# A decoder layer's last stage: late rows' gathers issued behind the second bulk tile, meta rows left out of the bulk, sample rows normed in sixteen pieces

## The reference

```
x = x + mixer(rmsnorm(x))                 # RWKV-7 branch, retention branch, w_out
x = x + hier_moe(rmsnorm(x))              # top-1 of 4 groups, then top-2 of its 4 experts
y = x * rsqrt(mean(x*x, -1) + 1e-6) * final_norm_g
return y[16:528], y[528:536], states      # the meta rows' y is dropped
```

## Time and profile before

| | us |
|---|---|
| median of 3 runs | 918.35 (917.46 to 920.85) |
| the profiled execution | 917.91 |
| its span, first to last instruction | 916.2 |
| last scatter-add to x issued | 876.40 |
| gathers of late rows issued | 884.13, 885.50, 886.83 |
| first sum of late rows starts (DVE) | 897.64 |
| PE's last matmul ends | 903.18 |
| last sum of late rows ends | 905.58 |
| last scatter to y issued | 911.23 |

### The profile page before, as it was taken

One profiled execution on the slowest core, in us unless ns is written; L12 is line 12 of the kernel. 1 busy time (PEld: TensorE's weight loads), 2 busy tenths in 40 slices (PEclk: granted clock), 3 DMA queues, 4 the chain that ended last, 5 costly groups with the idle time before them and its releaser, 6 DMA issues. The chain is left out here.

```text
span 916.2 us, 20394 instructions
## 1 busy us (share of the span) xinstructions
PE 854.0 (93%) x8958; PEld 599.6 (65%) x8958; DVE 376.7 (41%) x735; ACT 206.9 (23%) x427; POOL 37.6 (4%) x34
## 2 busy tenths in 40 slices
PE   8999999999999999999989989999999819999993
PEld 6877777788867766777767767766788613333330
DVE  6343334428955655444533324325511162111126
ACT  2101112033133232032123133212003230111125
POOL 0000000000000000000000000000000010222223
PEclk9999999999999999999999999999999958999998
DMA  9211111311311111110011201008272089999965
GB/s 355 107 46 46 47 46 47 150 48 70 112 47 49 55 36 38 36 37 29 26 35 49 94 26 47 28 2 299 86 298 92 0 283 415 396 395 393 391 221 208
DMA packets 27015, 118.75 MB, mean 130 GB/s; under 512 B 5344, under 2 KB 7648, under 8 KB 22064
## 3 DMA queue, kind: packets, MB, share of 16 engines
q1 hardware_dynamic: 22608, 106.51, 30.5%
q0 software_dynamic: 4320, 10.95, 4.1%
HBM read 104.17 MB, written 18.05 MB: 133 GB/s over the span
## 5 line engine op out<-in xcount | busy, mean ns | idle before, releaser
L884 PE MATMUL psum<-arena 128*128 128x268 f32 x1600 | 397.9, 397 | 2.7 <-ACT arena L1262 2.5
L884 PEld LDWEIGHTS psum<-arena 128*128 128x128 f32 x1600 | 295.4, 190 | 74.3 <-issue 7.9
L1453 DVE TENSOR_TENSOR arena<-psum,arena 128x256 f32<-128x256 f32 (+7 forms) x230 | 99.3, 437 | 280.5 <-PE psum L1201 57.8
L1262 ACT ACTIVATE arena<-psum 128x268 f32<-128x268 f32 (+9 forms) x181 | 72.7, 411 | 452.7 <-PE psum L884 280.3
L1453 DVE TENSOR_TENSOR arena<-arena 128x268 f32<-128x268 f32 (+10 forms) x203 | 102.0, 502 | 54.8 <-ACT arena L1262 43.4
L1201 PE MATMUL psum<-arena 128*128 128x268 f32 x384 | 90.3, 390 | 0.9 <-DVE arena L1453 0.9
L1998 PE MATMUL psum<-arena 128*32 128x512 f32 (+1 forms) x640 | 87.9, 613 | 2.9 <-DVE arena L2151 2.9
L1201 PEld LDWEIGHTS psum<-arena 128*128 128x128 f32 x384 | 71.3, 189 | 16.3 <-DVE arena L1453 1.7
L2151 DVE TENSOR_TENSOR arena<-psum,arena 128x256 f32<-128x256 f32 (+1 forms) x36 | 24.1, 691 | 109.6 <-ACT arena L2065 101.6
L1998 PEld LDWEIGHTS psum<-arena 128*32 128x32 f32 (+1 forms) x640 | 25.6, 118 | 61.7 <-issue 60.1
L1912 POOL DMA_INDIRECT arena<-u_rows,ids x12 | 12.4, 1036 | 809.7 <-DVE ids L2187 747.0
(11 more groups left out here) (190 smaller groups left out, 687.9 us busy)
## 6 DMA issues: line engine op xcount, KB each, us to landing
arena<-in_w_gu SPq DMA_DIRECT2D x16, 2048.0 KB, 20.7
arena<-in_w_in SPq DMA_DIRECT2D x46, 512.0 KB, 3.5
arena<-in_w_dn SPq DMA_DIRECT2D x16, 1024.0 KB, 18.7
arena<-in_w_out SPq DMA_DIRECT2D x2, 2048.0 KB, 11.9
arena<-in_x SPq DMA_DIRECT2D x8, 268.0 KB, 4.3
arena<-in_x SPq DMA_DIRECT2D x1, 2144.0 KB, 15.1
arena<-in_rets SPq DMA_DIRECT2D x1, 2048.0 KB, 15.9
out_rets<-arena SPq DMA_DIRECT2D x1, 2048.0 KB, 6.5
```

Source lines behind the costliest of these rows:

```text
L884: last = mm(ps, wt[:, i % NW, k, :], rhs[:, k, cols(hf)], start=(k == 0), stop=(k == nk - 1))
L1262: run(nc.scalar.activation(out, in_, fn, **kw), s)
L1453: run(v.tensor_tensor(out, a, b, op), s)
```

## The change

- Before the late gathers, POOL waits for the load of bulk tile 1.
- The bulk is rows 16 to 527 in four full tiles; tile 4 is now the 8 sample rows, each cut into 16 pieces of 64, so 128 partitions x 64. Its sum of squares is made per piece by ACT and added over the 16 pieces by one small matmul on PE with a block matrix `blk` (ones where two partitions belong to one row), into a column of bank 5, from which ACT takes the root. `blk` is made by DVE in `rt_in`; the matching pieces of final_norm_g come by one more load.
- The orders of squares (0, 1, 4, 2, 3, 5, 6, 7), of roots and norms (0, 1, 2, 3, 4, 5, 6, 7) and of the steps among them change, as below. The semaphore between the tiny table activations goes, and one of these (Sqrt, the third).
- POOL scatters tile 5 to y before `back(2)`.

```diff
@@ mixer: SP, ACT and DVE
+            sp.dma_start(g_smp, I["gfrow"][0:NB].rearrange("b (q c) -> (b q) c", q=16)).then_inc(d_ld, 16)
-                    act.wait_ge(d_ld, 48)
+                    act.wait_ge(d_ld, 64)
-                    dve.wait_ge(d_ld, 48)
+                    dve.wait_ge(d_ld, 64)
                     tt(quad, ident[:, 0:20], ident[:, 32:52], ALU.add)
+                    run(v.tensor_reduce(cnt, ident.rearrange("p (a b) -> p a b", a=NB), AX.X, ALU.add))
+                    run(v.tensor_copy(blk.rearrange("p (a b) -> p a b", a=NB), bc(cnt, P // NB)))
+                    run(v.memset(cnt, 0.0))
@@ final norm
+        SQUARED = [0, 1, 4, 2, 3, TT, TT + 1, TT + 2]
+        NORMED = [0, 1, 2, 3, 4, TT, TT + 1, TT + 2]
+        def bulk(t):
+            return xf[:, t, :] if t < TT - 1 else xf[:, t, 0:D // 16]
+        def bulk_rows(rows, t):
+            if t < TT - 1:
+                return rows[META + t * P:META + (t + 1) * P, :]
+            return rows[TP:T, :].rearrange("b (q c) -> (b q) c", q=16)
@@ SP
-                        n = rows_of(t)
-                        sp.dma_start(xf[0:n, t, :], x2_dram[t * P:t * P + n, :]).then_inc(z_x[t], 16)
+                        sp.dma_start(bulk(t), bulk_rows(x2_dram, t)).then_inc(z_x[t], 16)
@@ POOL
+                    then(z_x[1], 16, 16)
                     for j in range(LATE):
                         e = FIRST_LATE + j
                         pool.indirect_dma_start(late[:, j, :], None, x2_dram,
-                    for j in range(LATE):
+                    for j in range(LATE - 1):
                         back(j)
                     then(z_out[0], 48, 48)
                     then(z_out[1], 32, 32)
                     for j in range(LATE):
-                        then(z_y, TT + LATE, TT + j + 1)
+                        if j == 1:
+                            back(LATE - 1)
+                        then(z_y, TT + LATE, NORMED.index(TT + j) + 1)
@@ PE
                     hidden_in(NPASS - 1)
+                    at_least(pe, z_ss, TT + LATE, SQUARED.index(TT - 1) + 1)
+                    mm(bank(5)[:, 6 * NPASS:6 * NPASS + 1], blk, fs[:, TT - 1:TT], start=True, stop=True).then_inc(z_smp, 1)
                     down(NPASS - 2)
@@ ACT
-                    table(ACT.Sqrt)
+                    a(dummy, eps2[:, :], ACT.Sqrt)
                     for t in range(2):
                         square(t)
                         root(t)
-                    table(ACT.Sigmoid)
+                    a(lnx_eps, eps2[:, :], ACT.Sigmoid)
                     gate(NPASS - 1)
                     hidden_out(NPASS - 2)
-                    table(ACT.Sqrt)
+                    square(4)
                     square(2)
+                    hidden_out(NPASS - 1)
                     root(2)
-                    hidden_out(NPASS - 1)
-                    for t in range(3, TT + 2):
+                    square(3)
+                    root(3)
+                    root(4)
+                    for t in range(TT, TT + LATE - 1):
                         square(t)
                         root(t)
@@ DVE
                     summed(0)
                     normed(2)
                     normed(3)
+                    normed(4)
+                    normed(TT)
                     summed(1)
-                    normed(4)
+                    normed(TT + 1)
                     for q in range(2):
...
-                    for t in range(TT, TT + LATE):
-                        normed(t)
+                    normed(TT + LATE - 1)
```

More of the change, by code:

```diff
@@ L654, in hybrid_step @@
         assert top[0] <= base
+        blk = at(P)
+        g_smp = at(D // 16)
+        assert top[0] <= base
         top[0] = ug0
@@ L669, in hybrid_step @@
         u2b = at(2 * D, 2, D)
-        assert top[0] <= base, top[0] - base
+        assert top[0] <= ug0 + 4 * D
         oneb = E(nc.sbuf_tensor("oneb", [P, P], BF16))
@@ L1823, in hybrid_step @@
         z_x = [sem(f"z_x{t}") for t in range(TT)]
-        z_sq = sem("z_sq")
+        z_smp = sem("z_smp")
         z_ss = sem("z_ss")
@@ L1885, in _ @@
                     for t in range(TT):
-                        n = rows_of(t)
-                        sp.dma_start(xf[0:n, t, :], x2_dram[t * P:t * P + n, :]).then_inc(z_x[t], 16)
+                        sp.dma_start(bulk(t), bulk_rows(x2_dram, t)).then_inc(z_x[t], 16)
                     for t in range(TT):
-                        at_least(sp, z_y, TT + LATE, t + 1)
+                        at_least(sp, z_y, TT + LATE, NORMED.index(t) + 1)
                         sp.nop(nofuse=True)
-                        n = rows_of(t)
-                        sp.dma_start(O["y"][t * P:t * P + n, :], xf[0:n, t, :]).then_inc(z_out[t % 2], 16)
+                        sp.dma_start(bulk_rows(O["y"], t), bulk(t)).then_inc(z_out[t % 2], 16)
                     for j in range(LATE):
@@ L2080, in rows_out @@
                         a(yo[:, e % 2, :], psum[:, o:o + 1024], ACT.Copy, scale=w_s[:, e:e + 1]).then_inc(q_yo, 1)
-                    squares = [0]
+                    squares = []
                     def square(t):
-                        x = xf[0:rows_of(t), t, :] if t < TT else late[:, t - TT, :]
-                        n = x.shape[0]
+                        x = bulk(t) if t < TT else late[:, t - TT, :]
                         if t < TT:
@@ L2090, in square @@
                             at_least(act, z_add[t - TT], 1, 1)
[L2091 to L2096, removed]
-                    def root(t):
[L2099 to L2102, removed]
+                        if squares:
+                            at_least(act, z_ss, TT + LATE, len(squares))
+                        a(junk[:, 0:x.shape[1]], x, ACT.Square, scale=D ** -0.5, accum_out=fs[:, t:t + 1]).then_inc(z_ss, 1)
+                        squares.append(t)
+                        assert squares == SQUARED[:len(squares)]
+                    roots = []
+                    def root(t):
+                        roots.append(t)
+                        assert roots == NORMED[:len(roots)]
+                        if t == TT - 1:
+                            at_least(act, z_smp, 1, 1)
+                        else:
+                            at_least(act, z_ss, TT + LATE, SQUARED.index(t) + 1)
+                        a(rs[:, t:t + 1], bank(5)[:, 6 * NPASS:6 * NPASS + 1] if t == TT - 1 else fs[:, t:t + 1], ACT.Sqrt,
+                          bias=eps2[:, :]).then_inc(z_rt, 1)
                     for i in range(NPASS - 2):
@@ L2134, in _ @@
                     at_least(act, z_half, 1, 1)
-                    at_least(act, z_ss, TT + LATE, squares[0])
+                    at_least(act, z_ss, TT + LATE, len(squares))
                     a(junk[:, 0:512], x[:, 0:512], ACT.Square, scale=D ** -0.5,
@@ L2217, in hidden @@
                         tt(hh, b[:, FF:2 * FF], hh, ALU.mult, q_h)
-                    norms = [0]
+                    norms = []
                     def normed(t):
-                        norms[0] += 1
-                        x = xf[0:rows_of(t), t, :] if t < TT else late[:, t - TT, :]
+                        norms.append(t)
+                        assert norms == NORMED[:len(norms)]
+                        x = bulk(t) if t < TT else late[:, t - TT, :]
                         y = x if t < TT else fin[t - TT]
[L2225 to L2229, removed]
+                        at_least(dve, z_rt, TT + LATE, len(norms))
+                        v.reciprocal(rs[:, t:t + 1], rs[:, t:t + 1]).then_inc(z_rc, 1)
+                        at_least(dve, z_rc, TT + LATE, len(norms))
+                        v.scalar_tensor_tensor(y, x, rs[:, t:t + 1], g_smp if t == TT - 1 else g_row, ALU.mult,
+                                               ALU.mult).then_inc(z_y, 1)
                     def summed(j):
```

6 lines of the change are left out of this document (removed).

## The result

| | before | after |
|---|---|---|
| median (lowest to highest), 20 executions each | 918.90 (913.45 to 923.92) | 924.02 (918.39 to 926.97) |
| the profiled execution, its span | 917.91, 916.2 | 921.12, 917.9 |

The ratio is 1.0048, with a 95% interval of 1.0031 to 1.0066: the change costs 4.4 us, between 2.8 and 6.1. The forecast was +2.2 and 920.2, its range ended at 923.0, and the measured median lies 1.0 above it.

The account below looks back on a forecast made before the run. The prediction took the tail as bound by the late gathers, then DVE, then POOL, with PE off that path. 0.0 + 3.4 - 1.4 + 0.2 = +2.2 on 917.91 gave 920.1, stated as 920.2; range 917.2 to 923.0.

Parts of the forecast that it names:

- Term 1: Tail, moment when the three late gathers are in (T0): unchanged at 897.6, 0.0 us, between -2.3 and +2.0.
- Rival C: Late gathers end with the common DMA traffic, or tile 1 lands late: +1.0 to +2.0 us, 921.1 to 922.1; chance 0.15.
- Term 2: DVE from the late gathers' arrival to the end of the last sum: 11.37 us instead of 7.94, +3.4.
- Term 3: POOL from the end of the last sum to its last scatter: 4.26 us instead of 5.65, -1.4.
- Term 4: In `rt_in`, the new operations and the added load make PE lose 0.2 us (0 to 0.8).
- Rival D: In the tail, ACT gets stuck on tile 4's late load and DVE stands: 922.5 to 924.2; chance 0.13.
- Rival B: The free road wins: late gathers in at 895.3 to 896.6, -2.3 to -1.0 us, 917.9 to 919.1; chance 0.18.

Follow-up runs that it names:

- r8: The changed kernel with SP's bulk writes held until the three late gathers are in; ratio 1.0046 (1.0023 to 1.0069).
- r3: The changed kernel with DVE's norm 6 moved behind the two halves of the last sum; ratio 1.0041 (1.0011 to 1.0070).
- r16: Changed kernel with norms 2, 3 before the gathers, last `down` in other banks, bulk writes held, root 2 before `hidden_out(11)`, norm 4 behind sum(1); ratio 0.9989.
- r2: The changed kernel without POOL's wait for bulk tile 1; ratio 1.0026 (0.9997 to 1.0055).
- r6: The changed kernel with DVE's norms 2, 3 and 4 ahead of the wait for the gathers, and sum(1) before norm 5; ratio 1.0021 (0.9997 to 1.0044).
- r10: The kernel before, unaltered, for a further trace; no ratio given, 35.34 us from the last scatter-add to x to the last scatter to y.
- r1_after: The changed kernel again, unaltered; ratio to the kernel before 1.0027 (0.9999 to 1.0055).
- r11: The kernel before, unaltered, for a further trace; no ratio given, 34.13 us from the last scatter-add to x to the last scatter to y.
- r13: The changed kernel with the gathers waiting for bulk tile 0 instead of tile 1; ratio 1.0021 (0.9996 to 1.0047), one execution of 2944.52 us left out.

## Why the prediction was wrong, step by step

The forecast's sum for the tail was +2.2. With the means of the traces the tail is 38.10 against 34.13, +4.0, which agrees with the +4.4 (2.8 to 6.1) of the end-to-end times.

- **Term 1, T0: wrong; the step that failed is here.** Forecast 0.0 (-2.3 to +2.0), measured +2.4 (22.90 against 20.54). The step was "what the gathers lose by the wait they win back by the free road". They lose 6.2 us (the third is issued at 17.01 behind the mark on average, without the wait at 10.85) and win back 3.8 (5.88 from that issue to T0, without the wait 9.69). I had 5.9 and 5.9. Three errors make up the 2.4, and they add:
  - 0.7: the first gather went at 13.58, as forecast (13.6), but the third 0.7 later than forecast, since one issue of the three took 1.70 to 1.84 us. Held back, the gathers are issued beside DVE's norms 0 and 1; before, DVE had no norm there. No rival had this.
  - 1.0: the third landed 5.57 to 6.38 us behind its issue, where I had 4.9 (4.4, the fastest in the trace, and 0.5 for the output tiles). With the writes held it was still 4.75 (r8).
  - 0.7: I took 21.24 for the T0 of the kernel before, one trace, when four traces span 18.63 to 21.74 with a mean of 20.54.

  Rival C, with +1.0 to +2.0, came nearest in size, and its picture, gathers that end with the common traffic, fits the rows in which the DMA engines fall idle as they land. It was given 0.15. The Trainium skill's page "DMA: Bandwidth & Descriptors", section "Queues, rings and completion order", by which a completion waits for all earlier writes of its engine in whichever queue, points the same way; r8's shorter landing with the writes held agrees with it, and no run here shows the rule by itself.
- **Term 2, DVE's list: right.** Forecast +3.4, measured +3.45; the stall forecast as 1.6 was 1.54, norm 4's slot 0.4 was 0.39 (901.75 to 902.14). r3 shows that taking the stall and norm 6 away gives back 3.0 of X.
- **Term 3, POOL from X: right in sign, too small, and by another path.** Forecast -1.4, measured -1.90. I added up POOL's list and carried over 1.73 for `back(2)`; but those 1.73 were norm 5 holding up its issue, and in the changed kernel `back(2)` begins with DVE idle and takes 0.96. What sets the last scatter is norm 7: before, three norms stood behind X and norm 7 ended 4.50 behind it, now 2.61, and 1.13 to 1.15 follow in both, as in all traces but r16's. The prediction had that path too (X + 2.6 and 1.1), and called it no later than POOL's 4.26; it is the one that came, 3.74.
- **Term 4, `rt_in`: forecast +0.2, measured 0.0.** From its first step (the memset of `eps`) to PE's transposes it is 5.97 us after and 5.98 before. DVE's wait for the loads grew by 0.01 only, so the new operations fitted into the slack of 0.88.
- **Rival D** did not come in the changed kernel, its mechanism did in r2. **Rival B** fell: T0 was never under 21.89 with the wait.
- **The range.** By its own sum the end was 920.2 from a profiled run of 917.91. The 20 executions of before put their median at 918.90, 1.0 higher. That, and the 1.8 more in the terms, make up 2.8 of the 3.8 us by which the median lies above the forecast; the rest is within the interval of the ratio. The base was treated as exact, where one profile and three times were to be had; a margin of 1 us for it belonged into the range. The range reached to 923.0 for rival D's sake, which did not come; by term 1's own upper bound of +2.0, which was passed, the miss would have been larger. That the median lay only 1.0 above the range is luck.

## What to carry to other kernels

A wait put before a transfer that lies on the path has to win back the whole delay, and here it won 3.8 of 6.2 us. It pays only if what is let through first is on the path, and here the gathers were and the bulk tiles were not. Moving an issue in time also changes what runs beside it: look at what DVE does at the new place before taking over POOL's issue times from the old one. When late work depends on another engine's short chain (square, root), don't put it right behind its producer; put an independent step between, and check whether a step that is free on one engine is waited for by another (r16). Read a term that rests on shared DMA from several traces, for one trace may be 3 us off where the steps of one engine repeat to 0.01.

## What the runs showed of the hardware

- The mark varied from 872.96 (r6) to 881.17 (r10), with all code ahead of it alike but for `rt_in`. The granted clock of PE goes with it. Two stretches of the profiled execution after, and the same of r1_after (mark 874.75 and 879.06; columns as in the earlier trace rows, without a change in the code between the two):

```profile
460.00:480.00 20.00, 17.50 (x426) 12.99 (x424) 7.38 (x16) 6.01 (x11) 0.00 (x0) 1.00 0.07 16
620.00:640.00 20.00, 18.42 (x93) 13.22 (x92) 11.69 (x24) 5.74 (x8) 0.00 (x0) 1.00 0.99 361
```

```profile
460.00:480.00 20.00, 17.50 (x360) 12.86 (x349) 5.65 (x12) 6.01 (x11) 0.00 (x0) 0.83 0.06 16
620.00:640.00 20.00, 19.23 (x94) 13.47 (x92) 8.56 (x16) 4.05 (x6) 0.00 (x0) 0.85 0.90 319
```

PE is granted 1.00 in the first and 0.83 and 0.85 in the second. With the lower level at half of the upper, that is 6.8 and 6.0 us of each 20 at 1.2 GHz, in which 3.4 and 3.0 us of work at the full clock are lost. r10 and r11, the two latest marks, have 0.83 in both stretches too. Over the whole span the clock was granted at 0.978 in r6 and at 0.967 in r10. Other stretches count too: the profiled execution before has 1.00 in both of these and its mark at 876.40. That the clock makes single times of this kernel scatter by 9 us is argued from this; what decides the clock the runs don't show.
- After standing 2.8 to 3.1 us for `summed(0)`, the last `down` (32 matmuls) took 5.34 us (after), 6.58 (r1) and 4.99 (r3), but 3.64 in r6 after 3.8 us of standing, and 3.64 in r8 and r13 after 1.95 and 1.73.
- POOL's issue of an indirect DMA is held up by a norm of DVE that already runs (which reads rows in `arena` only): it ends 0.82 to 0.95 us behind the norm's end, and takes up to 1.85 us, where in the tail it otherwise takes 0.96 to 1.07 (86 and 76 issues in 18 traces). The late sums, of which one input comes from PE's banks (`psum`), don't do this. In the runs with the wait it meets the gathers: one or two of the three took 1.35 to 1.85 us in each of these runs, and none over 1.07 in those without it.
